# One inference step of a hybrid backbone with a top-4-of-32 MoE on one core: the layers in one straight program, each unit's W1 ahead of the preceding unit's W2, and the three units of four experts right behind the fixed pairs

## What is computed

```python
def _moe(h, p):
    logits = (t @ p['router_w'] + p['router_b'])
    top_v, top_i = lax.top_k(logits, TOP_K)          # 4 of 32
    combine = softmax(top_v) scattered to (tokens, 32)
    for each expert e:
        gu = t @ w1 + b1                             # 1024 -> 2 x 512
        gate, up = min(gu[:, :512], 7), clip(gu[:, 512:], -7, 7)
        acc += combine[:, e] * ((up + 1) * gate * sigmoid(1.702 * gate) @ w2 + b2)
```

## Time and profile before

| | us |
|---|---|
| median of 3 runs | 1728.8 (1727.98 to 1730.56) |
| the profiled execution, its own time | 1728.6 |
| its span | 1726.9 |
| TensorE busy (matmul) | 1556.0 (90%) |
| VectorE busy | 514.6 (30%) |
| ScalarE busy | 260.9 (15%) |
| granted TensorE clock, mean | 0.957 |
| HBM read | 542.03 MB, 315 GB/s over the span |

### The profile page before, as it was taken

How to read it: one execution, slowest core, us unless ns; L and a number is a source line. 1 busy time by engine, 2 the same in 40 slices (tenths; PEclk the granted TensorE clock), 3 DMA queues, 4 the chain that set the end, 5 groups by cost and what they waited for, 6 DMA issues and landing times. The chain is left out here.

```text
span 1726.9 us, 20608 instructions
## 1 busy us (share of the span) xinstructions
PE 1556.0 (90%) x8298; PEld 905.1 (52%) x8298; DVE 514.6 (30%) x1415; ACT 260.9 (15%) x585; POOL 3.8 (0%) x6
## 2 busy tenths in 40 slices
PE   3999999989999895986979999999899998959968
PEld 1756788765443442432447567887654433524424
DVE  1368336332211111111134583363322111111112
ACT  2144122020100000000021341220200000000001
POOL 0000000000000000000000000000000000000000
PEclk9999999999999997998989999999999999989979
DMA  9844713948999999999778447248579999999994
GB/s 336 294 159 144 295 69 130 355 187 321 419 419 412 428 426 428 427 427 427 317 261 313 150 152 269 70 156 324 218 298 412 420 412 427 428 427 428 428 427 200
DMA packets 100162, 545.80 MB, mean 316 GB/s; under 512 B 12704, under 2 KB 15520, under 8 KB 74976
## 3 DMA queue, kind: packets, MB, share of 16 engines
q1 hardware_dynamic: 90944, 539.92, 77.6%
q10 hardware_dynamic: 9120, 4.53, 1.1%
HBM read 542.03 MB, written 2.40 MB: 315 GB/s over the span
## 5 line engine op out<-in xcount | busy, mean ns | idle before, releaser
L849 PE MATMUL ps<-ring,arena 128*64 128x512 f32 (+1 forms) x1856 | 371.2, 632 | 50.4 <-DMA ring<-exp_w_dram 50.4
L849 PEld LDWEIGHTS ps<-ring,arena 128*64 128x64 f32 (+1 forms) x1856 | 111.9, 132 | 266.2 <-issue 266.2
L679 PE MATMUL ps<-hT,ring 128*128 128x256 f32 x768 | 171.4, 379 | 0.0
L873 PE MATMUL ps<-ring,arena 128*64 128x512 f32 (+1 forms) x736 | 161.9, 634 | 0.0
L679 PEld LDWEIGHTS ps<-hT,ring 128*128 128x128 f32 x768 | 144.1, 190 | 19.4 <-issue 1.0
L679 PE MATMUL ps<-arena,ring 128*128 128x256 f32 x640 | 144.6, 380 | 2.9 <-ACT arena L1143 1.6
L873 PE MATMUL ps<-arena 128*32 128x512 f32 (+1 forms) x384 | 98.2, 670 | 37.6 <-DMA ring<-exp_w_dram 37.6
L679 PEld LDWEIGHTS ps<-arena,ring 128*128 128x128 f32 x640 | 118.8, 190 | 19.0 <-issue 2.7
L827 PEld LDWEIGHTS ps<-arena 128*128 128x128 f32 x928 | 111.5, 197 | 23.5 <-issue 20.5
L640 PE MATMUL ps<-ring,hT 128*128 128x512 f32 (+1 forms) x320 | 119.7, 534 | 1.9 <-DVE hT L1307 1.9
L827 PE MATMUL ps<-arena 128*128 128x128 f32 x928 | 119.0, 283 | 2.6 <-DVE arena L1650 2.6
(11 more groups left out here) (282 smaller groups left out, 1345.4 us busy)
## 6 DMA issues: line engine op xcount, KB each, us to landing
ring<-exp_w_dram SPq DMA_DIRECT2D x151, 2048.0 KB, 20.6
arena<-exp_w_dram SPq DMA_DIRECT2D x44, 2048.0 KB, 15.6
ring<-ada_w_dram SPq DMA_DIRECT2D x24, 2048.0 KB, 8.2
ring<-w_in_dram SPq DMA_DIRECT2D x12, 2048.0 KB, 10.4
ring<-w_merge_dram SPq DMA_DIRECT2D x12, 2048.0 KB, 9.0
ring<-w_out_dram SPq DMA_DIRECT2D x4, 2048.0 KB, 11.1
ring<-w_o_lru_dram SPq DMA_DIRECT2D x2, 2048.0 KB, 7.9
ring<-w_o_mla_dram SPq DMA_DIRECT2D x2, 2048.0 KB, 19.6
```

Of the source, the lines that this page charges most:

```text
L679: last = mm(out, slot[:, k, cols], src[:, k, :], start=k == 0, stop=k == nk - 1)
L849: last = mm(ps[c, h, :], xTg[:, 4 * part + k, c], weights[i][:, k, h * 512:(h + 1) * 512], start=False, stop=True, skip_group_check=True)
L873: last = mm(ps[c, 2 + h, :], actT[:, f, c], weights[i][:, f, h * 512:(h + 1) * 512], start=f == 0, stop=f == 3)
```

## The change

- The setup block, the hardware loop over the layers, the clearing of the semaphores and the barrier go. One block holds both layers, written out twice in each engine's program. Semaphores count on from layer to layer (`now(l, s, v)`), or there is one for each layer (`in_layers`).
- `ada_w` is loaded by row blocks: each of the four slots holds 256 rows of all 2048 columns, in runs of 8 KB instead of 2 KB, and `ada_products` waits slot by slot. In layer 1 the norm stands between the first two and the last two slots.
- The second norm is spread over the output projection: chunk k - 1 of the norm behind chunk k of the projection, and the last one behind all.
- In the experts' part W2 of unit u - 1 stands behind W1 of unit u, and the scatter of u - 1 behind the transposes of u; gather and biases of a unit stand right ahead of its W1 (`dispatch`). The last W2 and scatter come at the end of the layer. `PARTS`, the buffers and the loads follow that order. The shared bias moves from unit 0 to unit 5.
- The order of units becomes pair, pair, quad, quad, quad, (96, 32), pair, and so on: three quads behind the two fixed pairs.
- Where an overflow unit has one expert only, W2 is loaded for both of its places (one part of 2 MB more in layer 0).

```diff
-UNITS = (pair_at(0), pair_at(2), ((4, 96), (31, 32)), pair_at(5), pair_at(7), quad_at(19), pair_at(9), pair_at(11),
-         quad_at(23), pair_at(13), pair_at(15), quad_at(27), pair_at(17))
+UNITS = (pair_at(0), pair_at(2), quad_at(19), quad_at(23), quad_at(27), ((4, 96), (31, 32)), pair_at(5), pair_at(7),
+         pair_at(9), pair_at(11), pair_at(13), pair_at(15), pair_at(17))
-PARTS = [(u, kind, i) for u, unit in enumerate(UNITS[:LOOPED]) for kind in range(3) for i in range(len(unit))]
+PARTS = []
+for _u in range(LOOPED):
+    PARTS += [(_u, kind, i) for kind in range(2) for i in range(len(UNITS[_u]))]
+    PARTS += [(_u - 1, W2, i) for i in range(len(UNITS[_u - 1])) if _u]
...
+        def load_ada(eng, layer, r, i, pos):
+            src = ada_w[bass.ds(layer, 1), 2 * P * i:2 * P * (i + 1), 2048 * r:2048 * (r + 1)]
+            eng.dma_start(ring[:, pos % RING, :].rearrange("p (k n) -> p k n", k=2),
+                          src.rearrange("o (k p) n -> p (o k) n", p=P)).then_inc(arr[pos % RING], 16)
...
+            for i, b in enumerate(LAST_SLOTS):
+                part_freed(last_user[b])
+                load_part(b, part_source(W2, expert_id(bass.ds(n_extra * 2 + (XT + i), 1))), more_arr[b - RING])
+            if l + 1 < L:
+                load_vectors(sp_, l + 1)
+                for kind in range(2):
+                    sp_.wait_ge(g1_mm[kind][l], n_extra + NU)
+                    for pos in LOOP_SLOTS[kind]:
+                        load_first(sp_, l + 1, pos)
...
+            def ada_products(r, bank, parts=range(4)):
+                for i in parts:
+                    slot = arrived(pe, l, S_ADA[r] + i).rearrange("p (k n) -> p k n", k=2)
+                    for k in range(2):
+                        for j in range(4):
+                            last = mm(ps[32 * j:32 * j + 32, bank, :], cT[:, 2 * i + k, :], slot[:, k, j * 512:(j + 1) * 512],
...
+            if l == 0:
+                pe.wait_ge(s_set[1], 16)
+                norm(0, 2, range(KC))
+                pe.wait_ge(s_set[4], 3)
+                ada_products(0, 0)
+            else:
+                ada_products(0, 0, range(2))
+                norm(0, 2, range(KC))
+                ada_products(0, 0, range(2, 4))
...
-                    merge(8)
-                    norm(1, 0)
+            for ch in range(KC):
+                merge(1)
+                if ch:
+                    norm(1, 0, [ch - 1])
+            norm(1, 0, [KC - 1])
...
+            def dispatch(q, first=False):
+                pe.wait_ge(disp, q + 1)
+                gather(range(KC))
+                ...
+                biases()
+                pe.wait_ge(xt_a, q + 1)
+                pe.wait_ge(xt_v, q + 1)
...
             for u in range(LOOPED):
                 experts = tiles(u)
+                dispatch(u, first=u == 0)
                 w1_products(u, 0, experts, part_weights(u, 0))
                 if u == 0:
                     table_parts()
                 w1_products(u, 1, experts, part_weights(u, 1))
                 if u == 0:
                     tables()
-                        pe.wait_ge(disp, u + 2)
-                        gather(range(6))
+                else:
+                    if u == 5:
+                        shared_bias()
+                    w2_products(tiles(u - 1), part_weights(u - 1, W2))
                 act_transposes(u)
-                        w2_products(u, experts, part_weights(u, 2))
+                if u:
+                    scatter(u, first=u == 1)
+                combine_transposes(u)
...
-            for i, s in enumerate(sems):
-                (nc.gpsimd, nc.vector, nc.scalar, nc.tensor, nc.sync)[i % 5].sem_clear(s)
-            nc.all_engine_barrier()
+        with nc.Block() as block:
+            @block.sync
+            def _(sp_):
+                ...
+                for l in range(L):
+                    sync_layer(sp_, l)
```

More of the change, by code:

```diff
@@ L126, in sb, with sem, now, in_layers @@
             return ctx.enter_context(nc.sbuf_tensor(name, shape, dt))
-        sems = []
-        def sem(name):
+        per_layer = {}
+        def sem(name, total):
             s = ctx.enter_context(nc.semaphore(name))
-            sems.append(s)
+            per_layer[s] = total
             return s
+        def now(l, s, v):
+            return s, l * per_layer[s] + v
+        def in_layers(name):
+            return [ctx.enter_context(nc.semaphore(f"{name}_of_{i}")) for i in range(L)]
         cst = sb("cst", [P, NC])
@@ L259, in build @@
         one_col = cst[:, C_ONE:C_ONE + 1]
[L262 to L276, removed]
@@ L307, in consumed @@
-        def consumed(pos):
+        arr = [sem(f"slot{s}_arrived", 16 * (later_uses(s) + 1 + len(PARTS) // BUFS)) for s in range(RING)]
+        more_arr = [sem(f"more{i}_arrived", 16 * (len(PARTS) // BUFS + 1)) for i in range(2)]
+        ld_lruw = sem("lruw_in", 32)
+        ld_ckv, ld_kr, ld_dk, ld_dv = (sem(n, 16) for n in ("cckv_in", "ckr_in", "cdk_in", "cdv_in"))
+        ld_rw, ld_b1, ld_b2 = sem("rw_in", 16), sem("b1_in", 32), sem("b2_in", 16)
+        ld_vec, ld_row = sem("vec_in", 16), sem("row_in", 16)
@@ L339, in rows_of @@
             return w[bass.ds(layer, 1), 0:nk * P, c0:c0 + nc_].rearrange("o (k p) n -> p (o k) n", p=P)
-        def ada_or_in(layer, pos):
-            for r in range(3):
-                if S_ADA[r] <= pos < S_ADA[r] + 4:
-                    return rows_of(ada_w, layer, KC, (4 * r + pos - S_ADA[r]) * 512, 512), 512
-            c0, w = IN_SLICES[S_IN.index(pos)]
-            return rows_of(w_in, layer, KC, c0, w), w
-        def load_early(eng, layer, pos):
-            src, w = ada_or_in(layer, pos)
-            eng.dma_start(ring[:, pos, 0:KC * w].rearrange("p (k n) -> p k n", n=w), src).then_inc(early[pos], 16)
@@ new lines, in load_in, with load_first @@
+        def load_in(eng, layer, pos):
+            c0, w = IN_SLICES[S_IN.index(pos)]
+            eng.dma_start(ring[:, pos % RING, 0:KC * w].rearrange("p (k n) -> p k n", n=w),
+                          rows_of(w_in, layer, KC, c0, w)).then_inc(arr[pos % RING], 16)
+        def load_first(eng, layer, pos):
+            if pos in S_IN:
+                load_in(eng, layer, pos)
+            else:
+                load_ada(eng, layer, 0, pos - S_ADA[0], pos)
+        def load_vectors(eng, layer):
+            eng.dma_start(vec[:, :], vecs[bass.ds(layer, 1), :, :].rearrange("o p n -> (o p) n")).then_inc(ld_vec, 16)
+            eng.dma_start(row[:, :], rows[bass.ds(layer, 1), :].broadcast_to((P, NR))).then_inc(ld_row, 16)
@@ L1787, in constants @@
+                for l in range(L):
+                    vector_layer(dve, l)
 def constants(np):
```

2493 lines of the change are left out of this document (1249 added, 1244 removed).

## The result

The changed kernel takes 1702.73 us (median of 4 runs, 1701.47 to 1703.85) against 1729.19 (4 runs, 1727.98 to 1730.56): ratio 0.9847, interval 0.9829 to 0.9864. The profiled execution of after took 1703.85 us, with a span of 1702.0.

A forecast was written before the change was run, and what follows sets the result against it. Quads were taken as bound by weight transfers, pairs and nearly all else by TensorE. Terms -5.9 + 1.6 - 0.9 - 11.4 + 1.6 - 0.9 - 1.5 = -17.4 gave 1711.4 us against the median; range 1703 to 1722.

The forecast's parts named there:

- Start: Kernel start to first input projection: projection begins at 35.2 instead of 43.06 us, 2.0 lost to the clock; gain 5.9 us.
- Second norm: Norm spread over the output projection, both layers: the root comes later, +1.6 us a layer, bounds +1 and +2.
- Experts, W1 ahead of W2: Pair units of the experts' part: no idle time to hide, so the new product order saves and costs nothing.
- Experts, order of units: Three quads moved to the front of the experts' part: nearly even, -0.9 us a layer, bounds -4 and +6.
- Between layers: Last scatter of layer 0 to the input projection: 14.6 instead of 27.04 us, gain 11.4, bounds 8 and 13.
- End: Last scatter to kernel end: squares, clearing and barrier go; gain 1.5 us, bounds 0 and 3.
- signs of being wrong: Pair units over 30.6 us, TensorE waiting for weights behind unit 5, or over 20 us between the layers.
- experts that don't come out even: Rival, experts' part: each layer 5 us longer rather than 0.9 shorter, 1723 us in all; chance 0.18.
- The slower clock: Rival, three quads in a row: TensorE at 1.2 GHz, 13 us a layer, 1737 us in all; chance 0.07.
- The long joint: Rival, between the layers: queued loads or a longer norm chain leave a gain of 5 us, 1718 in all; chance 0.07.
- Start and joint give more: Rival: gains of 10 us at the start, 13 between layers, 3 at the end, 1704 in all; chance 0.13.

The follow-up runs named there:

- short_runs: The changed kernel with `ada_w` loaded in runs of 2 KB as before, the product waiting for all four slots; 1711.05 us.
- norm_behind: The changed kernel with the second norm in one piece behind the output projection again; 1697.14 us.
- switch: The changed kernel with one tiny full-width product added between W1 and W2 of each unit; 1710.87 us, one run.
- no_switch: The changed kernel with the same tiny full-width product added ahead of the gather, where the array is already full-width; 1706.44 us, one run.
- order_alone: The kernel before with only the new order of units, three quads behind the two fixed pairs; 1732.8 us, ratio 1.0024 against the kernel before.
- quads_apart: The changed kernel with its quads at units 2, 5 and 8 instead of 2, 3 and 4; 1703.92 us.
- clear_end: The changed kernel with the semaphore clearing and a barrier added once, behind the last layer; 1705.17 us.
- unrolled: The kernel before with its hardware loop over the layers written out, clearing and barrier kept; 1723.01 us, ratio 0.9963 against the kernel before.
- changed_again: The changed kernel run once more with no edit; 1703.62 us.
- slots_all: The changed kernel, `ada_w` still in 8 KB runs, but each `ada_w` product waits for its last slot first; 1702.93 us, one run.

## Why the prediction came out as it did

- **Start: right.** -6.5 for -5.9. The projection began 1.0 us earlier than the 35.2 forecast, and ran 2.3 longer where 2.0 was taken off: the window 35 to 40 has a granted clock of 0.62, between the two levels of 1.2 and 2.4 GHz, behind a start in which the engine worked half of the time (16.20 of 34.24 us). The longer runs brought more than the 1.05 us that I took: the product begins at 29.64 in short_runs and at 27.43 in slots_all, 2.2 us, and 0.7 by the estimate from the Trainium skill, "DMA: Bandwidth & Descriptors", section "Why small descriptors are slow". The measurement decides; by the rates of 388 and 416 GB/s 1.5 of the 2.2 lies in the transfers. Whether their rate comes of the slow issue or of the packets, no run separates.
- **Second norm: right.** +2.0 for +1.6 a layer, at the upper bound of 2; norm_behind shows the 1.5 of it in the root itself. The rest is a slower product of the router, which had no term.
- **Experts, W1 ahead of W2: the step that failed.** It said that "the new order saves nothing", with bounds of 0 and 0.3 us a unit on the side of a loss only. A unit became 0.57 us shorter. The rows for it were there: I had W2 behind the gather at 7.02 and scatter behind W2 at 3.65, and took the length of a product for its own, though part of it (0.15 of W2's, by switch) belongs to what stands ahead of it. I carried 30.31 through seven units; at 29.74 they give 4.0 us in layer 0, and six of them 3.4 in layer 1, where the experts came 3.0 under the forecast. Of the 0.57, switch and no_switch show 0.27; for the rest the cause stays open, and only its place is known (scatter and gather). A small reading was off too: the transposes of a pair unit before are 0.72 and 0.22, and not 0.87, and the gather 3.77, and not 3.84, which moves no sum by more than 0.1 us.
- **Experts, order of units: right.** W2 of unit 4 began at 611.40, which is 615.9 with W1 of unit 0 at 383.01 as before, forecast 614.3, and W1 of unit 6 at 629.49 or 634.0, forecast 633.4. All waits for weights lie from unit 2 to W2 of unit 4, none behind. 634.0 + 7 x 29.74 instead of 633.4 + 7 x 30.31 explains 3.4 of the 3.5 us of layer 0. That the order in itself is nearly even order_alone and quads_apart show, but with opposite signs in the two kernels, which the sum doesn't give.
- **Between layers: the number right, its cause not named.** 14.60 us to the projection, forecast 14.6, with the clock taking 1.7 where 1.0 was taken off. I had worked out the new chain, which needs no account of the old one. Nearly a quarter of the old one, 6.4 us, was the jump of the hardware loop, which the prediction names nowhere.
- **End: mis-sized.** -3.3 for -1.5, outside its bounds (0 and 3). 2.5 is clearing and barrier, by clear_end.
- **Range.** Each bound of the unit's length was on the side of a loss, and so were the signs of being wrong: no pair unit over 30.6 us, no wait for weights behind unit 5 and no joint over 20 us came, and the forecast was still too long. The same 4 us a layer on the other side give 1711.4 - 8 = 1703.4, before start, joint or end give anything.

**The rivals.** The first one, experts that don't come out even, fell with the unit of 29.74 us. The slower clock fell: over 420 to 611 the granted clock is 0.82, but products behind a wait take about the 9.67 us of the earlier trace rows, and not twice their length:

```profile
572.24 9.98 PE L858 MATMUL ps<-ring,arena 128*32 128x512 f32 x64 [10.05 <-DMA ring<-exp_w_dram]
...
611.40 9.17 PE L858 MATMUL ps<-ring,arena 128*32 128x512 f32 x64 [2.68 <-DMA ring<-exp_w_dram]
```

These are 64 matmuls each, 7.07 us in full work (at 591.13 in after), so a product behind a wait loses up to 2.9, and this lies under the transfers, which go on at 427 GB/s. The long joint fell too. "Start and joint give more" came to 1704, near the time but not for its reason: start and joint gave what was forecast, and only the end gave more.

## What to carry to other kernels

A product's length in a trace depends on what stands ahead of it: when an order changes, look for the same product behind both kinds of neighbour before it is carried over unchanged, above all between packed and full-width products. When a joint of a hardware loop is priced, see whether the short program of an idle engine restarts well before the long ones; that gap was the jump here, and neither barrier nor clearing. Work that is laid among other work brings nothing where its last piece then stands uncovered: the norm interleaved with the projection cost 1.5 us a layer. And before a gain of 1 to 2 us is read from one trace, look whether the same product at the same place ran at full clock in one kernel and not in the other.

## What the runs showed of the hardware that was not expected

- The jump back over a layer of a hardware loop costs 6.1 to 6.4 us on TensorE, ScalarE and VectorE, and GpSimd starts 5.9 us before TensorE (unrolled, and "issue" in the chain of before); one barrier of all engines between layers costs 2.1.
- A pair of changes between products in 128\*64 tiles and full-width ones costs 0.27 us (switch against no_switch): W2 7.02 for 6.87 and a tiny product 0.34 for 0.14, less 0.08 on the gather.
- Issuing four loads of 2 MB takes SyncE 12.27 us in runs of 2 KB and 2.89 in runs of 8 KB.
- The input projection of layer 1 ran 20.02 us in after and 18.32 in norm_behind, though from the layer's first product to the projection it is 14.67 us in one (873.55 to 888.22) and 14.68 in the other (872.60 to 887.28). The window 888 to 898 of after shows 0.83 of the clock, 887 to 897 of norm_behind 1.00. TensorE had been busy 13.4 and 13.3 of the 16.5 us ahead of the projection. changed_again, quads_apart, clear_end and switch are as long there as after, slots_all as norm_behind. Why the clock is lower in one and not the other stays open; it is 1.7 us.
